# Two norms of latent attention joined in one double-wide root at the scan's end, and retention's products woven between the attention preparation

## The reference, cut to what matters

```python
h = rmsnorm(x) * (1 + scale1) + shift1
u = h @ w_in                 # split in three head groups
# SSD:       causal conv + silu, two-directional scan, y * silu(z), rmsnorm over 512
# retention: two-directional scan with fixed decays, group norm per head, * silu(g)
# MLA:       q_c = rmsnorm(u_q, 256) @ w_uq ; ckv = rmsnorm(u_kv, 128) ; kv = ckv @ w_ukv
#            rotary part on q and key of the latent tokens; softmax over 128 or 384 keys
x = x + gate1 * (concat(ssd, retention, mla) @ w_out)
x = x + gate2 * swiglu(rmsnorm(x) * (1 + scale2) + shift2)
# scale, shift, gate = silu(cond) @ w_ada + b_ada  (the "modulation")
```

## Time and profile before

| what | value |
|---|---|
| median of 3 runs | 1102.44 us (1101.33 to 1104.98) |
| the profiled execution | 1104.6 us, of which the span in the profile is 1102.7 us |
| TensorE busy | 1034.7 us, 94% of the span |
| VectorE, ScalarE, GpSimd busy | 632.0, 440.1, 98.3 us |
| chain that ended last | PE 86%, DVE 8%, ACT 3% |
| mean granted TensorE clock | 0.979 of full speed |
| the stage between scan and attention, first layer | 164.3 to 209.7 us |
| the same, second layer | 699.5 to 745.5 us |

### The profile page before, as it was taken

How to read it: one execution, slowest core, us unless ns; L and a number is a source line. 1 busy time by engine, 2 the same in 40 slices (tenths; PEclk the granted TensorE clock), 3 DMA queues, 4 the chain that set the end, 5 groups by cost and what they waited for, 6 DMA issues and landing times.

```text
span 1102.7 us, 16365 instructions
## 1 busy us (share of the span) xinstructions
PE 1034.7 (94%) x6520; PEld 942.9 (86%) x6520; DVE 632.0 (57%) x1138; ACT 440.1 (40%) x682; POOL 98.3 (9%) x99
## 2 busy tenths in 40 slices
PE   3999997899999999999999599889999999999996
PEld 2697994589999989999999589647899999999995
DVE  5567767657655544434356677685675545544333
ACT  3155446336433332333335444642563334333231
POOL 0003323003000000001000042400010000000010
PEclk9899999899999999999999899998999999999998
DMA  9642345313333468333353222550233333543431
GB/s 386 258 188 86 115 153 190 124 39 122 118 140 123 170 250 313 132 121 129 116 222 153 77 87 79 217 209 1 77 115 114 123 143 115 184 174 105 131 131 57
DMA packets 30679, 159.56 MB, mean 145 GB/s; under 512 B 3425, under 2 KB 4385, under 8 KB 19873
## 3 DMA queue, kind: packets, MB, share of 16 engines
q1 hardware_dynamic: 29328, 149.63, 37.4%
q10 hardware_dynamic: 1296, 9.18, 2.0%
HBM read 156.27 MB, written 2.52 MB: 144 GB/s over the span
## 4 chain that ended last, share of the span: by engine, by line
PE 86%; DVE 8%; ACT 3%; issue 1%; DMA 1%; POOL 0%; DVEq 0%; SPq 0%; ACTq 0%; POOLq 0%
PE ps L464 25%; PE ps L466 24%; PE ps L465 24%; PE ps L491 2%; DVE v L1441 2%; PE ps L865 1%; DVE wlo L1278 1%; PE ps L847 1%; PE ps L792 1%; ACT whi L966 1%; DMA x<-x_dram 1%; PE ps L662 1%; PE ps L856 1%; PE ps L684 1%; PE ps L710 1%
## 5 line engine op out<-in xcount | busy, mean ns | idle before, releaser
L464 PE MATMUL ps<-h_hi,whi 128*128 128x386 f32 (+1 forms) x1120 | 387.7, 346 | 0.2
L466 PE MATMUL ps<-h_hi,wlo 128*128 128x386 f32 (+1 forms) x1120 | 382.4, 341 | 0.0
L465 PE MATMUL ps<-h_lo,whi 128*128 128x386 f32 (+1 forms) x1120 | 381.5, 341 | 0.0
L1278 DVE TENSOR_TENSOR wlo<-stage,whi 128x2048 fp32r<-128x2048 f32 (+1 forms) x106 | 223.4, 2108 | 151.9 <-ACT whi L966 151.9
L966 ACT ACTIVATE whi<-stage 128x2048 fp32r<-128x2048 f32 (+1 forms) x106 | 185.9, 1753 | 228.1 <-PE ps L466 203.9
L464 PEld LDWEIGHTS ps<-h_hi,whi 128*128 128x128 f32 x1120 | 213.5, 191 | 11.1 <-issue 9.7
L465 PEld LDWEIGHTS ps<-h_lo,whi 128*128 128x128 f32 x1120 | 213.9, 191 | 0.3
L466 PEld LDWEIGHTS ps<-h_hi,wlo 128*128 128x128 f32 x1120 | 212.8, 190 | 0.1
L464 PE MATMUL ps<-hid_hi,whi 128*128 128x384 f32 x352 | 118.3, 336 | 0.0
L466 PE MATMUL ps<-hid_hi,wlo 128*128 128x384 f32 x352 | 118.3, 336 | 0.0
L465 PE MATMUL ps<-hid_lo,whi 128*128 128x384 f32 x352 | 118.3, 336 | 0.0
(11 more groups left out here) (269 smaller groups left out, 1147.2 us busy)
## 6 DMA issues: line engine op xcount, KB each, us to landing
stage<-wf_dram SPq DMA_DIRECT2D x44, 1024.0 KB, 4.8
adas<-wada_dram SPq DMA_DIRECT2D x80, 512.0 KB, 5.6
stage<-win_dram SPq DMA_DIRECT2D x22, 1024.0 KB, 4.8
stage<-wf_dram SPq DMA_DIRECT2D x32, 704.0 KB, 4.1
stage<-wout_dram SPq DMA_DIRECT2D x8, 1024.0 KB, 5.4
adaf<-wada_dram ACTq DMA_DIRECT2D x6, 1024.0 KB, 17.6
small<-small_dram SPq DMA_DIRECT2D x2, 1202.5 KB, 9.0
adas<-wada_dram ACTq DMA_DIRECT2D x2, 1024.0 KB, 29.9
```

What stands on the lines that cost most here:

```text
L464: mm(out, ah, bh, start=(k == 0), stop=False)
L465: mm(out, ah, bl, start=False, stop=False)
L466: return mm(out, al, bh, start=False, stop=(k == n - 1))
L1278: tt(wlo[:, g % 2, 0:width], stage[:, g % 2, 0:width], whi[:, g % 2, 0:width].bitcast(F32), ALU.subtract)\
```

## The change

One root of double width replaces the query's and the key's roots. Their squares are taken on ScalarE at the end of the scan, right after the copy-out of projection block 9, into `sq_b` (memory of the normed input, free once the last projection block is done). TensorE sums them in three products to PSUM banks 0 and 1 right after the scan's last products. ScalarE takes two logarithms and one exponential over 768 columns, before it loads the silu table; VectorE does the Newton step over 768 columns and scales the query, before it takes over the retention states. SSD's root follows later and reads squares in `sq_c`. There are thus five roots a layer instead of six, at an unchanged number of products.

TensorE's order changes: the four query products come before retention's last two state products; retention's scores and values of the three chunks lie between the rotation products, SSD's sum of squares and two modulation blocks; the group norm's two products come after the key and value products, the second one behind modulation block 5; blocks 6 and 7 follow directly, before attention. VectorE does both rotations before the second `ret_probs`, and the group norm's root last. The key's rotation works through bank 7 and `late` instead of bank 5 and a buffer of its own. SyncE's and GpSimd's instructions and their order stay the same.

```diff
-RSTD = 6
+RSTD = 5
...
+            sq_b, sq_c = (sb(n, [P, KD, TB], F32, place)[:, KW2:KD, 0:T] for n in ("sq_b", "sq_c"))
...
+            rt = late.rearrange("p (a t) -> p a t", a=2)
...
-                def mean_square(n, tiles):
-
-                    pe.wait_ge(gsq_ready, L * 4 + n)
-                    for m, src in enumerate(tiles):
-                        last = mm(ps[:, 7, 0:T], ones, src, start=(m == 0), stop=(m == len(tiles) - 1))
-                    last.then_inc(ms_ready, 1)
...
+                def ret_states(jobs):
+
+                    for s in jobs:
...
+                pe.wait_ge(gsq_ready, L * 4 + 2)
+                pe.wait_ge(u_raw if L else u_ready, 10)
+                for m in range(3):
+                    last = mm(ps[:, m // 2, 0:T], ones, sq_b[:, m, :], start=(m != 1), stop=(m != 0))
+                last.then_inc(ms_ready, 1)
+                ret_states((0, 1))
+                pe.wait_ge(ssd_y, L * 3 + 3)
+                ada_block(L * 6 + 3, 0, 2)
...
                     last.then_inc(q_ps, 1)
-
-                ada_block(L * 6 + 3, 6, 2)
-                pe.wait_ge(kr_ready, L * 3 + 3)
+                ret_states((2, 3))
+                pe.wait_ge(u_ready, L * N_WIN + N_WIN)
+                ret_scores(0)
+                mm(ps[hrow, 7, 0:LAT], perm, u[hrow, U_KR, CTX:T], start=True, stop=True).then_inc(krot_ps, 1)
+                ada_block(L * 6 + 3, 2, 2)
...
+                ret_values(0)
+                ret_scores(1)
+                pe.wait_ge(gsq_ready, L * 4 + 3)
+                pe.wait_ge(kr_ready, L * 3 + 3)
+                for m in range(4):
+                    last = mm(ps[:, 7, 0:T], ones, sq_c[:, m, :], start=(m == 0), stop=(m == 3))
+                last.then_inc(ms_ready, 1)
+                ret_values(1)
+                ret_scores(2)
+                ada_block(L * 6 + 3, 3, 2)
+                ret_values(2)
+                ada_block(L * 6 + 3, 4, 2)
 
                 pe.wait_ge(ck_ready, L * 3 + 3)
 
...
+                pe.wait_ge(ry_taken, L + 1)
+                for m in range(2):
+                    last = mm(ps[:, m, 0:T], cc(K_BD), ry[:, m, :], start=True, stop=True)
+                last.then_inc(mu_ps, 1)
...
+                ada_block(L * 6 + 3, 5, 2)
+                pe.wait_ge(q_ready, L * 2 + 2)
+                pe.wait_ge(centred, L + 1)
+                pe.wait_ge(gsq_ready, L * 4 + 4)
+                for m in range(2):
+                    last = mm(ps[:, 5 + m, 0:T], cc(K_BD), ry2[:, m, :], start=True, stop=True)
+                last.then_inc(ms_ready, 1)
+                ada_block(L * 6 + 3, 6, 2)
                 ada_block(L * 6 + 3, 7, 2)
-                pe.wait_ge(q_ready, L * 2 + 2)
...
+                            act.wait_ge(w_used, L * NB + N_WIN + 2)
+                            f(sq_b[:, 0:2, :], u[:, U_MQ:U_MQ + 2, :], ACT.Square).then_inc(gsq_ready, 1)
+                            f(sq_b[:, 2, :], u[:, U_CKV, :], ACT.Square).then_inc(gsq_ready, 1)
...
+                            act.wait_ge(ms_ready, L * RSTD + 2)
+                            act.wait_ge(rstd_ready, L * RSTD + 2)
+                            f(ny[:, 0, :], ps[:, 0, 0:T], ACT.Ln, bias=eps, scale=1.0 / RANKQ)
+                            f(ny[:, 1, :], ps[:, 1, 0:T], ACT.Ln, bias=eps, scale=1.0 / RANKKV).then_inc(ln_ready, 1)
+                            act.wait_ge(ln_ready, L * RSTD + 2)
+                            f(ny[:], ny[:], ACT.Exp, scale=-0.5).then_inc(y0_ready, 1)
...
-                act.wait_ge(ssd_gated, L * 2 + 2)
-                f(gsq[:], u[:, U_Z:U_Z + 4, :], ACT.Square).then_inc(gsq_ready, 1)
...
+                for h in range(HM):
+                    act.wait_ge(q_ps, L * HM + h + 1)
+                    f(qh[0:96, h, :], ps[0:96, h % 2, 0:T], ACT.Copy).then_inc(q_taken, 1)
+                act.wait_ge(ssd_gated, L * 2 + 2)
+                f(sq_c, u[:, U_Z:U_Z + 4, :], ACT.Square).then_inc(gsq_ready, 1)
                 split_hi(L, N_WIN + 1)
...
+                act.wait_ge(centred, L + 1)
+                f(ry2[:], ry[:], ACT.Square).then_inc(gsq_ready, 1)
+                rstd(L * RSTD + 4, ps[:, 5:7, 0:T], 2, 1.0)
...
+                n, y, t = nv[:], ny[:], nt[:]
+                dve.wait_ge(ln_ready, L * RSTD + 2)
+                for m, rank in enumerate((RANKQ, RANKKV)):
+                    ts(nv[:, m, :], ps[:, m, 0:T], -0.5 / rank, -0.5 * EPS, ALU.mult, ALU.add)
+                dve.wait_ge(y0_ready, L * RSTD + 2)
+                step(tt(t, y, y, ALU.mult))
+                step(tt(t, t, n, ALU.mult))
+                stt(n, t, 1.5, y, ALU.add, ALU.mult).then_inc(rstd_ready, 1)
+                dve.wait_ge(rstd_ready, L * RSTD + 3)
+                for m in range(2):
+                    q = u[:, U_MQ + m, :]
+                    stt(q, q, sc(C_QN + m), nv[:, 0, :], ALU.mult, ALU.mult).then_inc(qn_ready, 1)
                 ret_end(0)
                 ret_end(1)
+                for k0, t0, t1 in ((0, 0, CTX), (2 * P, CTX, T)):
+                    stt(ck[:, k0:k0 + t1 - t0], u[:, U_CKV, t0:t1], sc(C_KN), nv[:, 1, t0:t1], ALU.mult, ALU.mult)\
...
-                split_lo(L, N_WIN + 1)
-                rstd(L * RSTD + 2, ps[:, 7:8, 0:T], 1, 1.0 / (HS * 64))
-                for m in range(4):
-                    z = u[:, U_Z + m, :]
-                    stt(z, z, sc(C_SN + m), nv[:, 0, :], ALU.mult, ALU.mult).then_inc(mix_src, 1)
-                ret_probs(1)
-                dve.wait_ge(mix_src, L * 6 + 4)
-                rstd(L * RSTD + 3, ps[:, 7:8, 0:T], 1, 1.0 / RANKQ)
...
+                ret_probs(1)
+                split_lo(L, N_WIN + 1)
+                dve.wait_ge(qn_ready, L * 2 + 2)
+                dve.wait_ge(ck_ready, L * 3 + 3)
+                rstd(L * RSTD + 3, ps[:, 7:8, 0:T], 1, 1.0 / (HS * 64))
+                ret_probs(2)
+                for m in range(4):
+                    z = u[:, U_Z + m, :]
+                    stt(z, z, sc(C_SN + m), nv[:, 0, :], ALU.mult, ALU.mult).then_inc(mix_src, 1)
+                dve.wait_ge(ry_ps, L * 3 + 3)
+                nc.vector.tensor_copy(ry[:], ps[:, 0:2, 0:T]).then_inc(ry_taken, 1)
+                for m in range(4):
+                    mix_low(L, m, u[:, U_Z + m, :])
+                dve.wait_ge(mu_ps, L + 1)
+                dve.wait_ge(ry_taken, L + 1)
+                tt(ry[:], ry[:], ps[:, 0:2, 0:T], ALU.subtract).then_inc(centred, 1)
+                mixer_gates(L)
+                dve.wait_ge(mix_src, L * 6 + 4)
+                rstd(L * RSTD + 4, ps[:, 5:7, 0:T], 2, 1.0)
```

More of the change, by code:

```diff
@@ L245, in program @@
         x = sb("x", [P, KD, T])
+        with ExitStack() as place:
+            sq_b, sq_c = (sb(n, [P, KD, TB], F32, place)[:, KW2:KD, 0:T] for n in ("sq_b", "sq_c"))
         h_hi, h_lo = sb("h_hi", [P, KD, TB], F32R), sb("h_lo", [P, KD, TB], F32R)
@@ L326, in program @@
                 vm = sb("vm", [P, 4, 256], F32, part)
-                rt = sb("rt", [P, 2, LAT], F32, part)
+                sb("rotation_gap", [P, 2, LAT], F32, part)
                 qh = sb("qh", [P, HM, T], F32, part)
@@ L716, in _, with ret_scores @@
                         last.then_inc(y_ps, 1)
-                def mean_square(n, tiles):
-                    pe.wait_ge(gsq_ready, L * 4 + n)
-                    for m, src in enumerate(tiles):
-                        last = mm(ps[:, 7, 0:T], ones, src, start=(m == 0), stop=(m == len(tiles) - 1))
-                    last.then_inc(ms_ready, 1)
[L726 to L740, removed]
+                def ret_states(jobs):
+                    for s in jobs:
+                        c, d = STATE_JOBS[s]
+                        pe.wait_ge(kv_ready, L * 3 + max(c + 1, min(s + 1, 2)))
+                        pe.wait_ge(rvt_ready, L * 4 + s + 1)
+                        if s >= 2:
+                            pe.wait_ge(ret_state, L * 4 + s - 1)
+                        for r in range(HR):
+                            last = mm(ps[d * 64:d * 64 + 64, 5 + s % 2, r * 64:r * 64 + 64],
+                                      kvt[:, c, r * 64:r * 64 + 64], vtr[s % 2][:, r * 64:r * 64 + 64], start=True, stop=True)
+                        last.then_inc(rst_ps, 1)
+                def ret_scores(c):
                     if c:
@@ L747, in _, with ret_values @@
                     last.then_inc(rscore_ps, 1)
-                    if c:
-                        pe.wait_ge(rstd_ready, L * RSTD + 2 + c)
-                    mean_square(c + 1, ([gsq[:, m, :] for m in range(4)], [gsq[:, m, :] for m in range(2)],
-                                        [gsq[:, 2, :]])[c])
-                    ada_block(L * 6 + 3, 2 + c, 2)
+                def ret_values(c):
                     pe.wait_ge(rprob_ready, L * 3 + c + 1)
@@ L770, in _ @@
                 perm = const[hrow, K_PERM:K_PERM + NOPE + ROPE]
-                mm(ps[hrow, 5, 0:LAT], perm, u[hrow, U_KR, CTX:T], start=True, stop=True).then_inc(krot_ps, 1)
-                pe.wait_ge(ry_taken, L + 1)
```

(16 more changed lines are left out.)

48 lines of the change are left out of this document (10 added, 38 removed).

## The result

The changed kernel takes **1109.72 us** (median of 5 runs, 1108.68 to 1110.58) against 1102.8 for the kernel before on the same chip (5 runs, 1101.33 to 1104.98): ratio **1.0061, 95% interval 1.0047 to 1.0075**. It is slower by 6.9 us. The profiled execution took 1109.26 with a span of 1107.4.

What follows compares the result with a forecast made beforehand. TensorE, busy 94% of the span, was taken to bound the kernel, so only its idle or low-clock time counts. Chain +0.25, query clock +4.0 and attention clock +0.6 gave +4.85 on 1102.44: 1107.3, range 1101.0 to 1110.6.

Steps and rivals of the forecast that it cites:

- idle in one piece ahead of them: TensorE, done with two state jobs and two modulation blocks at 171.1, idles 4.0 us until the query products at 175.1.
- waits for chunks 1 and 2: TensorE waits about 1.0 us for chunk 1's probabilities and 2.4 for chunk 2's, replacing the old order's waits for roots.
- block 7's loads: Issued late, landing at the median 1.3 us before VectorE asks; as a rival, late loads give 1109.6, chance 0.1.
- The start: From the scan's last products at 166.62 through sums, joined root and query scaling to the query products at 175.1.
- The clock: Granted clock falls to 0.50 behind the 4.0 us idle stretch, costing 2.0 us a layer, 4.0 in both.
- The middle: From the query products on, VectorE's gapless queue of 13.1 us from chunk 0's `ret_probs` gives chunk 2's probabilities at 194.95.
- The end: From chunk 2's values through the group norm's wide root, 4.85 us and unhidden, to the first maximum at 210.85 against 210.43.
- chain term of +0.25: Shift of the first key maximum without clock effects: +0.4 us in the first layer, -0.15 in the second.
- Attention: Low clock may begin sooner in attention's first steps: 0 to 0.6 us a layer, taken as 0.3, in two layers 0.6.
- none above 2.2: Reading of the old stage between scan and attention: no single TensorE wait was longer than 2.2 us.
- the clock holds: Rival: the 4.0 us gap before the query products keeps clock 1.00, so only +0.85, 1103.3; chance 0.25.
- VectorE is early: Rival: last root ends before 207.9, needing chunk 2's probabilities by 192.6; about -4.2, 1098.2; chance 0.1.

Runs made afterwards that it cites:

- e3: The changed kernel with five unread 384-column products in the gap before the query products and GpSimd's decayed retention queries started earlier: 1106.79 us.
- e2: The changed kernel with GpSimd's decayed retention queries started behind the gating instead of the last states, the later four in another buffer: 1105.61 us.
- e4: The changed kernel's joined root with another order around it, two state take-overs before the root and other TensorE work in the gap: 1102.89 us.
- e9: e4 with unread products in attention's first steps and the mixing's four high halves between ScalarE's value copies; nothing unread in the query gap: 1096.94 us.
- e7: The kernel before with only seven unread 128-column products a layer, in attention's third and fourth step: 1098.81 us against 1103.29.
- e1: The changed kernel with five unread 384-column products a layer in TensorE's idle stretch before the query products: 1109.90 us.
- e5: e3 plus eight and ten unread 128-column products ahead of the values of chunks 1 and 2: 1104.94 us.

## Why the prediction was right, and where it wasn't

Forecast 1107.3, range 1101.0 to 1110.6, slower with 0.62; measured 1109.7. The difference was to be +4.85 and is +6.9 by medians, +6.8 by the marks. By its steps, in microseconds:

| step | forecast | measured |
|---|---|---|
| query products begin | +10.8 | +10.86 in both layers |
| idle in one piece ahead of them | 4.0 | 3.47 |
| clock in the query products, a layer | 2.0 | 1.69 (7.09 against 5.40) |
| first `ret_probs` | +17.56 | +19.61; +17.92 with the clock held |
| waits for chunks 1 and 2 | 1.0, 2.4 | 1.86, 2.30; 0.98, 2.31 in e3 |
| `ret_probs` 0 to values of chunk 2 | 13.1 | 14.3; 13.4 in e3; 13.0 in e2's first layer |
| from the second group norm's end to the maximum | 5.55 | 5.55 |
| low clock earlier in attention, a layer | +0.3 | -1.1 and -0.1 |
| block 7's loads | hidden | hidden |

**The start** was right to 0.1. TensorE was through with its blocks a little later, so the gap is shorter.

**The clock** was right in place and sign, 0.3 a layer too dear. Not in the forecast is the *second* fall in the first layer: from chunk 2's values to the second group norm it costs 1.6 (10.27 against 8.63 in the second layer). The wait of 2.4 that comes before it stood in the prediction, with no clock attached to it. By the Trainium skill's "TensorE: Matmul & The Clock Gate", Part 1, an idle gap puts the low clock back: the traces agree for three of the four gaps of 3.47 us (both layers of the changed kernel, the first of e2) and not for the fourth, which kept 1.00. They show falls behind waits of 2.3 as well.

**The middle** is the step that failed, in one term. VectorE's queue was costed by itself at 13.1, and GpSimd was checked only for whether it ends in time (8.8 us of room; it had them). But it runs beside exactly that queue, and the prediction put the cost of that at nothing. e2's first layer, with GpSimd out of the way, has 13.0 where the changed kernel has 14.3: 1.27 a layer, 2.5 in all. It is also why chunk 1 waited 1.86 instead of 1.0. The VectorE operation with an operand in PSUM (L1661, 0.42) isn't stretched, while two with both operands in SBUF are (L1662, L1663), and so is the copy within SBUF. This fits the page "SBUF — State Buffer" of the Trainium skill, section "SBUF: two separate sides": GpSimd and VectorE take a shared port pair in turn, each for a whole instruction. But not each such operation beside GpSimd is hit: L1673, both operands in SBUF, took 0.67 as in the kernel before.

**The end** was right: the group norm's wide root took 4.84 where 4.85 stood in the forecast. So was the chain term of +0.25. The first layer's maximum is 4.67 later than the forecast's +46.56 without the clock: query products 1.69, contention 1.27, second fall 1.64, which leaves 0.07. The second layer is 3.02 later: the same without the last, which leaves 0.06. Small errors on the way (0.36 too little up to the first `ret_probs`, 0.17 too much behind chunk 2's values) cancel.

**Attention** came out the other way, -1.2 in all instead of +0.6. Its low stretch begins and ends elsewhere; why it cost less isn't shown.

**The sum.** Measured +6.8 is 3.4 for the query products, 1.6 for the second fall, 2.5 for contention, 0.4 for the chain and -1.2 for attention. Two terms that the forecast put at nothing are worth 4.2; attention and the query products' clock, both too dear in it, gave 2.4 back. That the time fell into the range is in so far luck.

**The rivals.** Of "the clock holds" nothing was seen in this trace, though e2's second layer shows it can. "VectorE is early" needed chunk 2's probabilities by 192.6 and had them at 196.4, in a trace whose scan ended 1.7 earlier: on the prediction's scale at 198.2. The loads of block 7 were waited for (0.81 and 0.65 by TensorE), yet the block ended at 212.04, before VectorE's last root at 213.17, so they cost nothing.

What stays open: the part of e2's gain (1.9 of 4.1) that its trace doesn't show; and what decides between two equal gaps. Equal idleness was followed by either clock: 3.47 us in e2's two layers, 2.7 in e4 and e9 against before's second layer, 2.0 in e7 against before. The prediction's "none above 2.2" was read in the first layer; the second layer of before waits longer once, and keeps the clock:

```profile
709.37 0.71 PE L745 MATMUL ps<-u 64*128 64x128 f32 x8 [2.73 <-DVE small L1602]
710.00:712.00 2.00, 2.00 (x8) 1.25 (x7) 0.69 (x1) 1.95 (x4) 1.61 (x3) 1.00 0.96 391
```

## What to carry to other kernels

Gathering an engine's short waits into one long one didn't help here, because its granted clock fell behind the long one: give such a fall a chance and not a fixed price. Cost the gaps that come *after* as well, since the clock held in e1 and e3 fell at the next ones. When a step moves, list what the other engines do at the new time: a helper that is "in time" may still lengthen the queue that everyone waits for. And before work is moved in such a stage, try a few products that nobody reads in the gaps; seven small ones a layer were worth 4.5 us in the old kernel, while no new order without such products (the changed kernel, e2, e4) was faster than before. But end them before the wait ends: in e5 they ran 0.8 past it in each layer.

## What the runs showed of the hardware

- Two idle stretches of 3.47 us in one execution, same code in both layers: granted clock 0.50 behind the first (products 7.09 us), 1.00 behind the second (5.40).
- Behind the gaps of 2.7 us in e4 and e9 the clock was 0.50 in all four cases (8.32, 6.89, 6.80 and 7.09 us for 5.40 of work). Behind the wait of 2.73 in the second layer of the kernel before it stayed 1.00.
- A wait of 2.00 in e7 was followed by 0.50 in both layers, the same wait (1.99) in the kernel before by 1.00 in both.
- With seven unread products of 128 columns per layer in attention's third and fourth step (e7) the clock was 1.00 there: -2.5 us a layer.
- GpSimd beside VectorE, both on operands in SBUF: VectorE's operations 0.41 to 0.69, 0.42 to 0.75, 1.22 to 1.55, 0.68 to 1.01, and one unchanged (0.67); GpSimd's four 2.77 to 4.54.
